# Hybrid decoder trunk, two layers, one core: order of the input projections, waits of the attention products, and GpSimd's entry into the last expert stage

## What is computed

```
h = rmsnorm(x)
q, k, v, pz, gu, gv, g = split(h @ w_in)
ya = sliding_window_attention(q, k, v) @ w_branch_a
yb = multiscale_pool(pz) @ w_branch_b
yc = (gelu(gu) * spatial_mix(rmsnorm(gelu(gv)))) @ w_branch_c
x  = x + (sigmoid(g0)*ya + sigmoid(g1)*yb + sigmoid(g2)*yc) @ w_out
x  = x + peer_ffn(rmsnorm(x))
```

## Time and profile before

| | |
|---|---|
| median of 3 runs | 2143.91 us |
| the profiled execution's own time | 2144.6 us |
| its span | 2142.8 us |
| TensorE busy | 2086.6 us, 97% of the span |
| VectorE, ScalarE, GpSimd busy | 1520.0, 976.5, 778.6 us |
| TensorE's share of the chain that ended last | 95% |
| mean granted clock of TensorE | 0.993 |
| memory traffic | 191 GB/s over the span |

### The profile page before, as it was taken

How to read it: one execution, slowest core, us unless ns; L and a number is a source line. 1 busy time by engine, 2 the same in 40 slices (tenths; PEclk the granted TensorE clock), 3 DMA queues, 4 the chain that set the end, 5 groups by cost and what they waited for, 6 DMA issues and landing times.

```text
span 2142.8 us, 45777 instructions
## 1 busy us (share of the span) xinstructions
PE 2086.6 (97%) x14382; PEld 1943.4 (91%) x14382; DVE 1520.0 (71%) x3212; ACT 976.5 (46%) x1363; POOL 778.6 (36%) x323
## 2 busy tenths in 40 slices
PE   7999999999999999999989999999999999999997
PEld 6999899999998888899889999999999988888996
DVE  3753159789878888777648431797989788886776
ACT  4644454554543333344355444545554433333443
POOL 5698669500000000244367986793000000003442
PEclk9999999999999999999999999999999999999999
DMA  7355457655557777655453554576555687776553
GB/s 234 123 184 183 157 169 227 217 163 161 162 193 245 239 241 242 205 189 185 166 170 127 187 187 149 179 230 203 162 163 160 210 243 241 241 242 194 183 189 120
DMA packets 154706, 410.71 MB, mean 192 GB/s; under 512 B 16987, under 2 KB 67340, under 8 KB 154588
## 3 DMA queue, kind: packets, MB, share of 16 engines
q1 hardware_dynamic: 154220, 407.75, 59.9%
q0 software_dynamic: 368, 1.57, 0.2%
HBM read 382.00 MB, written 27.26 MB: 191 GB/s over the span
## 4 chain that ended last, share of the span: by engine, by line
PE 95%; ACT 1%; DVE 1%; issue 1%; DMA 0%; DVEq 0%; ACTq 0%
PE bank L1048 55%; PE bank L1245 32%; PE bank L1297 5%; PE bank L1223 1%; PE bank L1070 1%; PE bank L1146 0%; PE bank L1103 0%; PE bank L1207 0%; DVE area L748 0%; DVE hT L755 0%; DVE act L976 0%; PE bank L1144 0%; DVE coef L980 0%; DMA x<-in_x 0%; ACT area L485 0%
## 5 line engine op out<-in xcount | busy, mean ns | idle before, releaser
L444 POOL TENSOR_TENSOR halves<-ring,halves 128x1024 fp32r<-128x1024 f32 x308 | 772.4, 2520 | 1327.3 <-ACT halves L509 1325.5
L1048 PE MATMUL bank<-hT,halves 128*128 128x256 f32 x8688 | 1120.6, 285 | 10.8 <-DVE hT L755 9.0
L509 ACT ACTIVATE halves<-ring 128x1024 fp32r<-128x1024 f32 x668 | 707.3, 1060 | 888.0 <-PE bank L1048 468.7
L1048 PEld LDWEIGHTS bank<-hT,halves 128*128 128x128 f32 x8688 | 1068.3, 191 | 18.8 <-issue 9.8
L1245 PE MATMUL bank<-halves,coef 128*128 128x512 f32 x3072 | 711.7, 391 | 3.8 <-DVE coef L982 3.8
L1245 PEld LDWEIGHTS bank<-halves,coef 128*128 128x128 f32 x3072 | 573.3, 188 | 122.6 <-DVE coef L982 5.9
L943 DVE TENSOR_TENSOR halves<-ring,halves 128x1024 fp32r<-128x1024 f32 x360 | 438.9, 1220 | 61.0 <-ACT x L649 25.7
L976 DVE TENSOR_TENSOR act<-act,area 128x256 f32<-128x256 f32 x256 | 223.8, 874 | 99.6 <-ACT act L619 93.9
L956 DVE TENSOR_SCALAR onehot<-ids,x 128x128 f32<-128x128 f32 x512 | 173.7, 339 | 1.9 <-issue 1.9
L1297 PE MATMUL bank<-onehot,x 128*128 128x128 f32 x1024 | 156.0, 274 | 0.0
L955 DVE TENSOR_SCALAR x<-ids,x 128x128 f32<-128x128 f32 x512 | 143.1, 279 | 16.9 <-PE bank L1297 15.9
(11 more groups left out here) (137 smaller groups left out, 951.9 us busy)
## 6 DMA issues: line engine op xcount, KB each, us to landing
ring<-in_stream SPq DMA_DIRECT2D x672, 512.0 KB, 3.5
held_blocks<-act SPq DMA_DIRECT2D x188, 128.0 KB, 1.9
act<-held_blocks SPq DMA_DIRECT2D x188, 128.0 KB, 3.1
area<-rel_scratch SPq DMA_DIRECT2D x2, 1024.0 KB, 6.4
rel_scratch<-act POOLq DMA_DIRECT2D x1, 1532.0 KB, 14.5
area<-in_consts SPq DMA_DIRECT2D x2, 576.0 KB, 3.8
x<-in_x SPq DMA_DIRECT2D x1, 1024.0 KB, 5.0
out_y<-x SPq DMA_DIRECT2D x2, 512.0 KB, 2.7
```

The lines of the kernel that those rows point to most:

```text
L444: pool.tensor_tensor(halves[:, s, 1, :], ring[:, s, :], halves[:, s, 0, :].bitcast(F32), ALU.subtract)\
L509: a.activation(halves[:, s, 0, :], ring[:, s, :], ACT.Copy).then_inc(hi_done, 1)
L1048: i = pe.matmul(o, stationary[a], moving[b], start=begin and n == 0, stop=end and n == len(TERMS) - 1)
```

## The change

Three things are altered.

1. In the stream and in all programs, k and v (tiles 2 and 3) stand in front of q (tiles 4 to 7), and gv (tiles 12 to 15) in front of gu (tiles 16 to 19). In ScalarE's program the squares and the root of gelu(gv) move with gv, in front of the roundings of tiles 19 to 22 and of gelu of gu.
2. The transposes of block 1 are grouped by pair of heads (h and h+4), as the attention products need them. The single wait for all six copies is replaced by one wait in each of the four attention groups, for the copies up to its own.
3. GpSimd waits, before its first subtraction of the last stage, until the coefficients of block 95 are ready.

```
-T_Q = T_PARAM + 2
-T_K = T_Q + QC
+T_K = T_PARAM + 2
 T_V = T_K + 1
-T_PZ = T_V + 1
-T_GU = T_PZ + GROUPS
-T_GV = T_GU + GROUPS
-T_MIX = T_GV + 4
+T_Q = T_V + 1
+T_PZ = T_Q + QC
+T_GV = T_PZ + GROUPS
+T_GU = T_GV + 4
+T_MIX = T_GU + GROUPS
...
@@ gpsimd
+                pool.wait_ge(coef_ready, l * NK + EARLY)
                 low(T_MU, 0, l)
...
@@ scalar
+                high_up_to(T_V + 3)
+                b = group("kv")
+                a.activation(kT, b[:, 0:S], ACT.Copy)
+                a.activation(v_tok, b[:, S:].rearrange("p (t c) -> p t c", t=TT), ACT.Copy).then_inc(taken_a, 1)
                 for n in range(2):
                     high_up_to(T_Q + 2 * n + 1 + 3)
                     b = group("q")
...
-                high_up_to(T_V + 3)
-                b = group("kv")
...
-                    high_up_to(T_GU + 2 * blk)
+                    high_up_to(T_GV + 2 * blk)
...
-                for n in range(2):
-                    high_up_to(T_GU + 2 * n + 1 + 3)
-                    b = group("gu")
-                    a.activation(uT[:, 2 * n:2 * n + 2, :], b[:, :].rearrange("p (c t) -> p c t", c=2),
-                                 ACT.Gelu_apprx_tanh).then_inc(taken_a, 1)
                 for t in range(TT):
                     high_up_to(T_GV + 3 + 3)
                     b = group("gv")
                     a.activation(gv[:, t, :], b[:, :], ACT.Gelu_apprx_tanh).then_inc(taken_a, 1)
-                a.wait_ge(taken_a, l * NGA + taken_before(first("pT0"))[1])
+                a.wait_ge(taken_a, l * NGA + taken_before(first("gu"))[1])
...
+                for n in range(2):
+                    high_up_to(T_GU + 2 * n + 1 + 3)
+                    b = group("gu")
+                    a.activation(uT[:, 2 * n:2 * n + 2, :], b[:, :].rearrange("p (c t) -> p c t", c=2),
+                                 ACT.Gelu_apprx_tanh).then_inc(taken_a, 1)
...
@@ tensor
...
-                        i = pe.transpose(b[:, u * P:(u + 1) * P], lg1[:, 2 * n + u // 2, (u % 2) * P:(u % 2 + 1) * P], ident)
+                        i = pe.transpose(b[:, u * P:(u + 1) * P], lg1[:, n + 4 * (u // 2), (u % 2) * P:(u % 2 + 1) * P], ident)
                     i.then_inc(groups_done, 1)
-                pe.wait_ge(taken_a, l * NGA + taken_before(first("attn"))[1])
                 for c in range(QC):
+                    pe.wait_ge(taken_a, l * NGA + taken_before(first("pT1") + c + 1)[1])
                     b = group("attn")
...
-                            i = pe.matmul(b[:, u * S + P:(u + 1) * S], v_tok[:, sblk, :], pT1[:, 2 * h + sblk, :],
+                            i = pe.matmul(b[:, u * S + P:(u + 1) * S], v_tok[:, sblk, :], pT1[:, 4 * c + 2 * u + sblk, :],
```

More of the change, by code:

```diff
@@ L113 @@
 PLAN = (
-    [("h1T", "V")] * 4 + [("q", "A")] * 2 + [("kv", "A")] + [("lg0", "V")] * 2 + [("lg1", "V")] * 4
-    + [("pz", "V")] * 2 + [("gu", "A")] * 2 + [("gv", "A")] * 2 + [("pT0", "A")] * 2 + [("pT1", "A")] * 4
+    [("h1T", "V")] * 4 + [("kv", "A")] + [("q", "A")] * 2 + [("lg0", "V")] * 2 + [("lg1", "V")] * 4
+    + [("pz", "V")] * 2 + [("gv", "A")] * 2 + [("gu", "A")] * 2 + [("pT0", "A")] * 2 + [("pT1", "A")] * 4
     + [("attn", "A")] * 4 + [("gmlp", "V")] * 2 + [("pool", "V")] * 2
@@ L549, in _ @@
                         .then_inc(taken_a, 1)
-                high_up_to(T_V + 3)
-                b = group("kv")
-                a.activation(kT, b[:, 0:S], ACT.Copy)
-                a.activation(v_tok, b[:, S:].rearrange("p (t c) -> p t c", t=TT), ACT.Copy).then_inc(taken_a, 1)
                 for blk, lg in ((0, lg0), (1, lg1)):
-                    high_up_to(T_GU + 2 * blk)
+                    high_up_to(T_GV + 2 * blk)
                     a.wait_ge(max_ready, l * 2 + (blk + 1))
@@ L1079, in _ @@
                 pe.wait_ge(scaled, l * 4 + 1)
[L1080 to L1084, removed]
                 b = group("kv")
-                columns(T_K, b[:, 0:S])
+                columns(T_K, b[:, 0:S], l * 4 + 2)
                 w = tile(T_V, KD)
@@ L1094, in _ @@
                 i.then_inc(groups_done, 1)
+                for n in range(QC // 2):
+                    b = group("q")
+                    for c in range(2):
+                        i = columns(T_Q + 2 * n + c, b[:, c * S:(c + 1) * S])
+                    i.then_inc(groups_done, 1)
                 pe.wait_ge(taken_a, l * NGA + 3)
@@ L1105, in _ @@
                         i.then_inc(groups_done, 1)
[L1106 to L1111, removed]
+                for n in range(GROUPS // 2):
+                    b = group("pz")
+                    for c in range(2):
+                        i = columns(T_PZ + 2 * n + c, b[:, c * S:(c + 1) * S])
+                    i.then_inc(groups_done, 1)
                 b = [group("gv") for _ in range(TT)]
@@ L1125, in _ @@
                                 i.then_inc(groups_done, 1)
+                for n in range(GROUPS // 2):
+                    b = group("gu")
+                    for c in range(2):
+                        i = columns(T_GU + 2 * n + c, b[:, c * S:(c + 1) * S])
+                    i.then_inc(groups_done, 1)
                 pe.wait_ge(probs_ready, l * 2 + 1)
@@ L1371, in lay_out @@
         par[:, C_BSP:C_BSP + GROUPS * P] = inp["b_spatial"][l].reshape(1, -1)
-        o[T_PARAM:T_Q] = par.reshape(P, 2, TILE).transpose(1, 0, 2)
-        o[T_Q:T_K] = cols(w[:, order], 0, QC)
-        o[T_K:T_PZ] = cols(w, n_q, 2)
+        o[T_PARAM:T_K] = par.reshape(P, 2, TILE).transpose(1, 0, 2)
+        o[T_Q:T_PZ] = cols(w[:, order], 0, QC)
+        o[T_K:T_Q] = cols(w, n_q, 2)
         c0 = n_q + 2 * n_kv
-        o[T_PZ:T_GU] = cols(w, c0, GROUPS)
-        o[T_GU:T_GV] = cols(w, c0 + GROUPS * P, GROUPS)
+        o[T_PZ:T_GV] = cols(w, c0, GROUPS)
+        o[T_GU:T_MIX] = cols(w, c0 + GROUPS * P, GROUPS)
         c0 += 2 * GROUPS * P
-        o[T_GV:T_MIX] = w[:, c0:c0 + GROUPS * P].reshape(2, 4, P, 2, S).transpose(3, 0, 2, 1, 4).reshape(4, P, TILE)
+        o[T_GV:T_GU] = w[:, c0:c0 + GROUPS * P].reshape(2, 4, P, 2, S).transpose(3, 0, 2, 1, 4).reshape(4, P, TILE)
         c0 += GROUPS * P
```

## The result

The changed kernel takes 2126.22 us, median of 4 runs (2125.79 to 2126.62), against 2144.06 before (4 runs): a ratio of 0.9916, 95% interval 0.9903 to 0.9928. The forecast was 2125.9. The profiled execution took 2125.79 us at a span of 2124.0, 18.8 less than before; the sum had said 18.0.

What follows compares the result with a forecast made beforehand. TensorE, busy 97% of the span, was taken as the bound, so only its gaps and slow stretches count. Terms 11.83 + 0.14 + 6.04 = 18.0 us off the median 2143.9 gave 2125.9 us, range 2122.5 to 2132.0.

Steps and rivals of the forecast that it cites:

- the sum: All gains together: 11.83 + 0.14 + 6.04 = 18.0 us off the profiled span of 2142.8.
- Attention, 2 x 5.92: TensorE's gap before the attention products and the slow stretch behind it: 4.19 + 1.73 = 5.92 us gained a layer.
- 1.73 for the clock: Eight attention head products take 5.36 us at full clock instead of 7.09, so 1.73 us a layer is gained.
- The rival of a clock that falls anyway: Attention slowed in both layers as now: 3.5 us lost, 2129.4 us; chance 15%.
- the third copy comes in time: ScalarE's third copy, needed by the first attention group, is done at about 2.3 us, before the transposes end at 2.6.
- What is late next: Around the attention, VectorE's signals, ScalarE's rounding of tile 19 and one more table load per layer move closer; all stay hidden.
- The rival of a full ScalarE queue: Squares, root and loads end 2.0 us past the margin, delaying tile 19 or VectorE's scaling: 2129.9 us; chance 7%.
- the drain behind a table load: The Trainium skill's 1.38 us per ScalarE table switch; by it rounding 19 would be about 2.0 us late each layer.
- k and v in front of q, 0.07 a layer: Wait before the logits becomes one copy of q instead of two of k and v: 0.14 us gained in all.
- GpSimd, 2.25 and 3.79: Start of the last stage: without TensorE's gap for coefficient 95, 2.25 us gained in layer 0, 3.79 in layer 1.
- The slower case: GpSimd falls out of step for the whole last stage, 0.63 us per block, 40 us in all: 2166; chance 2%.
- 1.9 us to chance at a layer's start: A slow-clock stretch at a layer's start may be lost or won, 1.9 us either way.

Runs made afterwards that it cites:

- gap filled: Kernel before, with 18 identity products put into TensorE's gap between the transposes and the attention: 2141.43 us, ratio 0.9981.
- order only: Changed kernel with the single wait for all six copies and GpSimd's old entry put back, so only the tile order differs from before: 2136.2 us, ratio 0.9951.
- waits only: Kernel before, with only the transposes grouped by pair of heads and one wait per attention group, on the old order: 2140.29 us, ratio 0.9974.
- GpSimd only: Kernel before, with only GpSimd's wait for coefficient 95 before its first subtraction of the last stage: 2141.02 us, ratio 0.9977.
- second only: Kernel before, with the wait for coefficient 95 in front of GpSimd's second subtraction of the last stage: 2141.15 us, ratio 0.9984.
- two more squares: Changed kernel with two more squares of gelu(gv) on ScalarE in front of the root, some 1.1 us: 2129.74 us.
- order and GpSimd: Changed kernel with the single wait for all six copies and the old grouping of the transposes put back: 2129.79 us, ratio 0.9928.
- logits in pairs: Changed kernel with the logits of token block 0 in four groups of two heads: 2128.09 us, ratio 0.9923.
- two filled kernels: Changed kernel with identity products where TensorE idles before a layer's transposes: 2127.13 us; the same plus block 0's logits in four groups of two heads: 2126.10 us.

## Why the prediction was right

**Attention, 2 x 5.92.** Measured 5.92 and 5.93 (A). Its pieces hold singly: the gap, and 1.73 for the clock against 1.70 in the kernel with the gap filled (1.63 in the attention itself; its first product is 0.1 slower behind a wait). The rival of a clock that falls anyway didn't come: 1.00 through the whole stretch. That the third copy comes in time and later groups don't wait is shown by the row without brackets.

**What is late next.** VectorE's margin of 1.0 and ScalarE's of 0.8 us came out as worked out. The rival of a full ScalarE queue falls, and with it the drain behind a table load: the row of the next instruction begins as the load ends, three times in this stretch.

**k and v in front of q, 0.07 a layer.** The wait fell from 0.75 to 0.69 us. As small as said.

**GpSimd, 2.25 and 3.79.** B fell by 2.46 and 3.82, and by 2.3 and 3.8 with this part alone. The mechanism is shown by the wait in front of the second subtraction. But 1.5 us of layer 1's share was not a property of the kernel: of eight gaps of 1.93 us profiled (before, order only, waits only, gap filled) only two had the low clock behind them. By an estimate from B in the profiles without it, this part is worth 4.5 to 5 us in most executions rather than 6.0; the medians with it alone differ by 4.2. The term was the one profile's, and that the sum agrees with the difference of two single profiles to 0.8 us is in part luck.

**The slower case.** GpSimd did not fall out of step. In the steady part of the last stage VectorE's product is as long, and as idle before, as in the earlier trace rows:

```profile
892.70 2.35 DVE L977 TENSOR_TENSOR act<-act,area 128x256 f32<-128x256 f32 x1 [1.34 <-ACT act L620]
```

**What went unforeseen.** Of the remaining 0.8 us of the profile, 0.46 lie at the start of layer 0, in front of its first product of halves, which the change does not touch; 0.24 lie in B and 0.18 behind the last u(96). The prediction gave 1.9 us to chance at a layer's start. The runs show up to 7. A changed kernel measured in such executions would have left the range of 2122.5 to 2132.0 (one of nine did, with 2133.58); the range was too narrow for that.

## What to carry to other kernels

Price a gap of the busiest engine with what follows it: here 4 us of idle time cost 5.9. Where two engines share a port, order them by who is awaited: one instruction of the engine with time to spare, put some 2 us later, took a stall away. And when the total scatters by more than the effect, compare stretches between two fixed points of the program.

## What the hardware showed

- Behind the gap of 4.04 us the attention was slow in 6 of 6 cases (before, GpSimd only, second only; 6.90 to 7.09 us); behind 1.08 and 2.58 us in 0 of 6; but behind gaps of 1.93 us before a v product in 2 of 8, and behind a wait of 0.7 us the logits were slow in 2 of 24 (7.34 and 7.23 us, in GpSimd only and second only). The length of the gap alone doesn't say whether the clock falls; what else decides stays open.
- The low clock can stay on while TensorE is busy without a gap: 0.50 from 26.2 to 39.0 us in one execution, and the same in two others (order only, two more squares). What brings it is not shown. The idle times in front were much the same in executions without it (order and GpSimd, logits in pairs: 1.00 from 20.7 to 24.8 us). The two filled kernels didn't have the long stretch, but still had 0.65 and 0.64 in their first products of halves, behind an idle time of 4.15 and 2.26 us that the filling leaves.
- Turning from one layer to the next takes TensorE 2.1 to 2.4 us behind its last product, in which the profile shows no wait. It shows only when the idle time around it is filled, in the two profiles of filled kernels.
